# Opening of a two-layer encoder trunk: order of the first loads, first projection by token tiles, TensorE kept running on the identity

## The reference, cut to what matters

```python
# x (1, 512, 1024) float32; two layers, each: mixer, residual + layer norm, SwiGLU, residual + layer norm
proj = h @ even_w_in[0]                                   # (512, 2048): the first work
qa, ka, va, ub = jnp.split(proj, [512, 1024, 1536], axis=-1)
oa = chunk_band_attention(qa, ka, va, even_rel_bias[0])
ob = s5_mixer(ub, lam_re, lam_im, b_re, b_im, c_re, c_im, d_skip, log_dt, glu_w, glu_b)
#   dt = exp(log_dt); mag = exp(lr*dt); ar = mag*cos(li*dt); ai = mag*sin(li*dt) ... (per state)
mix = jnp.concatenate([oa, ob], axis=-1) @ even_w_out[0]
...
# layer 1: stick-breaking attention in the mixer's place
```

## Time and profile before

| | us |
|---|---|
| median of 3 runs | 1211.2 (1210.94 to 1211.3) |
| profiled execution, its own time | 1211.29 |
| span of the profiled execution (first to last instruction) | 1209.5 |
| TensorE busy | 1188.7 |
| ScalarE busy | 423.2 |
| VectorE busy | 409.7 |
| GpSimd busy | 522.2 |

### The profile page before, as it was taken

One profiled execution on the slowest core, in us unless ns is written; L12 is line 12 of the kernel. 1 busy time (PEld: TensorE's weight loads), 2 busy tenths in 40 slices (PEclk: granted clock), 3 DMA queues, 4 the chain that ended last, 5 costly groups with the idle time before them and its releaser, 6 DMA issues.

```text
span 1209.5 us, 14969 instructions
## 1 busy us (share of the span) xinstructions
PE 1188.7 (98%) x6221; PEld 970.2 (80%) x6221; DVE 409.7 (34%) x661; ACT 423.2 (35%) x577; POOL 522.2 (43%) x270
## 2 busy tenths in 40 slices
PE   7999999999999999999999999999999999999996
PEld 6877768988888888888887777778988888888885
DVE  8369462811101110000804777758211111110007
ACT  6345674332323222122225555533323222221220
POOL 6897514344444444444343222214444444444440
PEclk9999999999999999999999999999999999999998
DMA  8622315253333333233253121111633333233311
GB/s 210 184 78 68 97 66 196 67 142 98 105 88 104 87 105 104 88 105 89 62 163 87 53 70 53 53 33 56 174 93 99 91 101 104 88 105 92 101 52 70
DMA packets 152642, 117.30 MB, mean 97 GB/s; under 512 B 18688, under 2 KB 138536, under 8 KB 152576
## 3 DMA queue, kind: packets, MB, share of 16 engines
q1 hardware_dynamic: 152576, 116.36, 32.8%
HBM read 112.00 MB, written 3.17 MB: 95 GB/s over the span
## 4 chain that ended last, share of the span: by engine, by line
PE 93%; DVE 4%; ACT 1%; DMA 1%; issue 0%; SPq 0%; POOL 0%; DVEq 0%; ACTq 0%
PE ps L1480 18%; PE ps L1482 17%; PE ps L1481 17%; PE ps L1502 9%; PE ps L1504 9%; PE ps L1503 9%; PE ps L1901 2%; PE ps L1927 2%; PE ps L1912 1%; PE ps L1510 1%; PE ps L1718 1%; PE ps L1729 1%; PE ps L1945 1%; DVE stats L1353 1%; PE ps L1659 1%; PE ps L1947 1%
## 5 line engine op out<-in xcount | busy, mean ns | idle before, releaser
L571 POOL TENSOR_TENSOR wlo<-raw,whi 128x1024 fp32r<-128x1024 f32 x189 | 454.3, 2408 | 630.8 <-ACT whi L674 629.9
L1480 PE MATMUL ps<-xhi,whi 128*128 128x512 f32 (+1 forms) x1000 | 379.6, 380 | 0.0
L1482 PE MATMUL ps<-xhi,wlo 128*128 128x512 f32 (+1 forms) x1000 | 374.4, 374 | 0.0
L1481 PE MATMUL ps<-xlo,whi 128*128 128x512 f32 (+1 forms) x1000 | 374.3, 374 | 0.0
L674 ACT CAST whi<-raw 128x1024 fp32r<-128x1024 f32 x189 | 199.9, 1063 | 207.9 <-PE ps L1504 180.8
L1480 PEld LDWEIGHTS ps<-xhi,whi 128*128 128x128 f32 x1000 | 188.5, 188 | 41.0 <-issue 6.4
L1482 PEld LDWEIGHTS ps<-xhi,wlo 128*128 128x128 f32 x1000 | 188.4, 188 | 33.8
L1481 PEld LDWEIGHTS ps<-xlo,whi 128*128 128x128 f32 x1000 | 188.6, 189 | 32.3
L1022 DVE TENSOR_TENSOR gt<-ps,sg 128x512 f32<-128x512 f32 x44 | 30.4, 692 | 372.6 <-PE ps L1482 372.6
L1502 PE MATMUL ps<-whi,ghi 128*128 128x512 f32 x352 | 137.1, 390 | 0.0
L1504 PE MATMUL ps<-whi,glo 128*128 128x512 f32 x352 | 137.0, 389 | 0.0
(11 more groups left out here) (219 smaller groups left out, 1071.3 us busy)
## 6 DMA issues: line engine op xcount, KB each, us to landing
raw<-in_ffn_w SPq DMA_DIRECT2D x132, 512.0 KB, 3.8
raw<-in_odd_w_in SPq DMA_DIRECT2D x24, 512.0 KB, 3.8
raw<-in_even_w_in SPq DMA_DIRECT2D x16, 512.0 KB, 4.6
h<-in_x SPq DMA_DIRECT2D x8, 512.0 KB, 5.0
raw<-in_even_w_out SPq DMA_DIRECT2D x8, 512.0 KB, 3.6
raw<-in_odd_w_out SPq DMA_DIRECT2D x8, 512.0 KB, 3.5
bias<-rel_scratch SPq DMA_DIRECT2D x8, 256.0 KB, 4.2
out<-h SPq DMA_DIRECT2D x3, 512.0 KB, 2.6
```

What stands on the lines that cost most here:

```text
L571: eng.tensor_tensor(lo, raw_of(b), hi, ALU.subtract).then_inc(w_lo, 1)
L1480: eng.matmul(o_, w_hi_, x_hi_, start=start, stop=False)
L1481: eng.matmul(o_, w_hi_, x_lo_, start=False, stop=False)
L1482: return eng.matmul(o_, w_lo_, x_hi_, start=False, stop=stop)
```

## The change

On SyncE the first weight block is the first load, then the four x tiles; the loads of lambda and dt move to ScalarE's queue. TensorE makes 18 transposes of the identity matrix into a free PSUM bank before the first x tile. The x tiles use other PSUM banks (0, 1 for tiles 0 and 2; 4, 5 for tiles 1 and 3), so that the first projection can begin, in quarters of 128 tokens, before tile 3 is turned. ScalarE rounds block 0 and the x tiles before it makes Sin. VectorE's xlo operations stand earlier among the parameter operations. The whole diff:

```diff
--- before.py
+++ after.py
@@ -37,6 +37,7 @@
 RAW = 3
 WS = 5
 TAIL = 4
+WARM = 18
 
 ALU = mybir.AluOpType
 ACT = mybir.ActivationFunctionType
@@ -372,7 +373,7 @@
         angles, turns = psf[:, 4 * S:4 * S + PAIRS * NC], psf[:, 0:PAIRS * NC]
 
         def turned_at(n, t):
-            return 0 if n == 0 and t == 3 else 2 * t * S
+            return t % 2 * 4 * S if n == 0 else 2 * t * S
 
         def piece_cols(t, w):
             return t[:, 0:2 * w].rearrange("p (h x) -> p h x", h=2)
@@ -416,13 +417,8 @@
                     issued[0] += 1
 
             xt = x[0].rearrange("(t p) d -> t p d", p=P)
-            eng.dma_start(pl[:, 7, :], lam_re[0].rearrange("(a b) p -> a (b p)", b=2)).then_inc(lam_landed, 16)
-            eng.dma_start(pl[:, 8, :], lam_im[0].rearrange("(a b) p -> a (b p)", b=2)).then_inc(lam_landed, 16)
-            eng.dma_start(dt2[:], log_dt[0].rearrange("(a b) -> a b", b=2)).then_inc(lam_landed, 16)
-            eng.dma_start(h[:, 0, :], xt[0]).then_inc(x_landed[0], 16)
-            eng.dma_start(h[:, 1, :], xt[1]).then_inc(x_landed[1], 16)
             weights_upto(1)
-            for t in range(2, NT):
+            for t in range(NT):
                 eng.dma_start(h[:, t, :], xt[t]).then_inc(x_landed[t], 16)
             weights_upto(3)
             eng.dma_start(bnr[:], b_re[0].rearrange("(a b) p i -> (b p) a i", b=2)).then_inc(b_landed, 16)
@@ -691,21 +687,24 @@
                 eng.copy(xhi[:, :, t * P:(t + 1) * P],
                          psf[:, c:c + D].rearrange("p (k n) -> p k n", k=KT)).then_inc(x_hi, 1)
 
+            eng.dma_start(dt2[:], log_dt[0].rearrange("(a b) -> a b", b=2)).then_inc(lam_landed, 16)
+            eng.dma_start(pl[:, 7, :], lam_re[0].rearrange("(a b) p -> a (b p)", b=2)).then_inc(lam_landed, 16)
+            eng.dma_start(pl[:, 8, :], lam_im[0].rearrange("(a b) p -> a (b p)", b=2)).then_inc(lam_landed, 16)
             act.wait_ge(lam_landed, 48)
             eng.activation(dt2[:], dt2[:], ACT.Exp).then_inc(dt_ready, 1)
+            first_upper(0)
             act.wait_ge(m_ready, 1)
             eng.activation(pl[:, 4, :], pl[:, 9, :], ACT.Exp, scale=float(L)).then_inc(mag_ready, 1)
             eng.activation(scratch(MAG_), pl[:, 9, :], ACT.Exp).then_inc(mag_ready, 1)
+            first_upper(1)
+            rounded[0] = 1
+            upper_x(0, 0)
+            upper_x(0, 1)
+            upper_x(0, 2)
+            upper_x(0, 3)
             act.wait_ge(arg_ready, 1)
             eng.activation(pl[:, 16, :], pl[:, 12, :], ACT.Sin).then_inc(trig_ready, 1)
             eng.activation(pl[:, 17, :], pl[:, 13, :], ACT.Sin).then_inc(trig_ready, 1)
-            upper_x(0, 0)
-            first_upper(0)
-            upper_x(0, 1)
-            first_upper(1)
-            rounded[0] = 1
-            upper_x(0, 2)
-            upper_x(0, 3)
             upper_upto(1)
 
             def project_out(n, dst, scale=None):
@@ -1076,6 +1075,7 @@
             link(eng.tensor_scalar(q_(RS), q_(TH), PI_BELOW, -PI_BELOW, ALU.min, ALU.max))
             link(eng.scalar_tensor_tensor(out=q_(RC), in0=q_(RS), scalar=-1.0, in1=q_(RS), op0=ALU.mult, op1=ALU.min))
             eng.tensor_scalar(q_(RC), q_(RC), math.pi / 2, None, ALU.add).then_inc(arg_ready, 1)
+            lower_x(0, 0)
             count(tt(q_(A), q_(LR), q_(LR), ALU.mult))
             count(tt(q_(B), q_(LI), q_(LI), ALU.mult))
             count(eng.tensor_scalar(q_(T), q_(TH), L / (2 * math.pi), ROUNDER, ALU.mult, ALU.add))
@@ -1083,19 +1083,18 @@
             settle()
             count(tt(q_(A), q_(A), q_(B), ALU.add))
             link(eng.tensor_scalar(q_(T), q_(T), ROUNDER, None, ALU.subtract))
+            lower_x(0, 1)
             count(eng.reciprocal(q_(A), q_(A)))
             link(less(q_(TH8), q_(T), TWO_PI_1, q_(TH8)))
             link(less(scratch(TH8_), q_(T), TWO_PI_REST, q_(TH8)))
             count(eng.tensor_scalar(scratch(TURN8_), scratch(TH8_), 1 / (2 * math.pi), None, ALU.mult))
-            lower_x(0, 0)
-            lower_x(0, 1)
             settle()
             both = ps[0:PAIRS, 7, 2 * P:4 * P].rearrange("p (a b) -> p a b", a=2)
+            lower_x(0, 2)
             link(eng.tensor_copy(turn_hi[:], both))
             tt(turn_lo[:], both, turn_hi[:].bitcast(F32), ALU.subtract).then_inc(ramp_ready, 1)
 
 
-            lower_x(0, 2)
             lower_x(0, 3)
             dve.wait_ge(mag_ready, 2)
             dve.wait_ge(trig_ready, 2)
@@ -1556,16 +1555,17 @@
                     if half == 0:
                         mm.then_inc(acc_half, 1)
 
-            def project_half(half):
+            def project_quarter(t):
                 wh, wl = (w[:, 0, :].rearrange("p (k n) -> p k n", k=KT) for w in (whi, wlo))
-                c = slice(half * 2 * P, (half + 1) * 2 * P)
+                c = slice(t * P, (t + 1) * P)
+                pe.wait_ge(x_ready, t + 1)
                 for k in range(KT):
-                    if half == 0 and k == 0:
+                    if t == 0 and k == 0:
                         pe.wait_ge(first_lo, 1)
-                    if half == 0 and k == KT // 2:
+                    if t == 0 and k == KT // 2:
                         pe.wait_ge(w_lo, 1)
                     mm = three(ps[:, 2, c], wh[:, k], wl[:, k], xhi[:, k, c], xlo[:, k, c], k == 0, k == KT - 1)
-                if half:
+                if t == NT - 1:
                     mm.then_inc(w_used, 1)
 
             def project(n, b):
@@ -1575,22 +1575,28 @@
                 mm.then_inc(w_used, 1)
 
             pe.wait_ge(const_ready, 1)
-            for t in range(NT):
+            for i in range(WARM):
+                eng.transpose(ps[:, 3, 0:P], ident[:], ident[:])
+            for t in range(2):
                 pe.wait_ge(x_landed[t], 16)
-                if t == 3:
-                    pe.wait_ge(x_ready, 1)
                 turn(0, t)
-            pe.wait_ge(x_ready, 2)
-            project_half(0)
+            pe.wait_ge(x_ready, 1)
+            pe.wait_ge(x_landed[2], 16)
+            turn(0, 2)
+            project_quarter(0)
+            project_quarter(1)
+            pe.wait_ge(x_landed[3], 16)
+            turn(0, 3)
+            project_quarter(2)
             pe.wait_ge(ramp_ready, 2)
-            pe.wait_ge(x_ready, NT)
-            for row, into in enumerate((angles, turns)):
+            for row, into in ((1, turns), (0, angles)):
+                if row == 0:
+                    project_quarter(3)
                 for half in range(2):
                     c = slice(half * S, (half + 1) * S)
                     eng.matmul(into[:, c], turn_hi[:, row, :], ramp[:, c], start=True, stop=False)
                     mm = eng.matmul(into[:, c], turn_lo[:, row, :], ramp[:, c], start=False, stop=True)
             mm.then_inc(angle_done, 1)
-            project_half(1)
             pe.wait_ge(pl_ready, 1)
             for i in range(5):
                 mm = eng.transpose(ps[:, 6, i * PAIRS:(i + 1) * PAIRS], pl[:, i, :], ident[0:PAIRS, 0:PAIRS])
```

## The result

The changed kernel takes 1228.98 us as the median of four runs (1223.74 to 1232.3), the kernel before 1211.24 beside it: a ratio of 1.0143, with an interval of 1.0125 to 1.016. It is 17.7 us slower. The forecast was 1212.4, its range ended at 1215.6: the prediction is wrong, and by much more than either slow rival would explain. Slower was forecast and slower it is, but for another reason, so that much was luck. The profiled run is the shortest of the four, 1223.74 with a span of 1221.9, so its trace explains 12.45 us over the profiled run of before; the rest of the 17.7 is taken up further down.

What follows compares the result with a forecast made beforehand. TensorE, busy 98% of the span, was taken as the bound. The opening's saved 1.4 us become a wait for block 1, and late block 4 delays the third projection: +1.2 us on 1211.3 gives 1212.4, range 1210.5 to 1215.6.

Steps and rivals of the forecast that it cites:

- either slow rival: Clock stays low in the opening (1215.4 us, chance 0.20), or a 128-column matmul costs 0.11 us (1214.6, chance 0.10).
- The late block 1: Weight block 1's rest on GpSimd ready at 23.0, so the second projection starts at 23.05 against 22.88.
- A matmul of 128 columns: I take 0.067: First projection on TensorE: each 128-column matmul takes 0.067 us, a quarter 1.6 us; bounds 0.06 and 0.11.
- The rival with 0.11: First projection: a 128-column matmul costs 0.11 us, a quarter 2.7, 2.2 more than forecast, 1214.6 us; chance 0.10.
- first with a high clock from the start of the x tiles: TensorE's opening: clock at the high level from the x tiles on, their transposes 0.109 us each from about 6.5.
- The rival of the low clock: TensorE's opening: everything up to about 15 runs at half speed, 4.2 us, 1215.4 us; chance 0.20.
- Small loads on ScalarE's queue ... free: Lambda and dt loads: Exp of dt starts near 3.5 instead of 3.2, costing nothing; bounds nothing and 2 us.
- VectorE: rest of tile 0 8.75 to 9.95: VectorE's opening: rest of x tile 0 made from 8.75 to 9.95, six operations following, tile 1 ready at 12.4.
- the step that counts: TensorE turns x tile 3 only after quarter 1, to 15.0, though it has lain there since 10.4.
- the copy behind block 4: ScalarE copies the first projection after rounding block 4; third projection starts at 29.7 against 28.49, TensorE losing 1.2 us.

Runs made afterwards that it cites:

- e4: The changed kernel with each quarter as two steps of 64 columns, 192 matmuls for block 0: 1252.81 us, one run.
- e6: The kernel before with only the new order of loads, the three small loads on ScalarE's queue: 1215.14 us.
- f2: The kernel before, halves of 256 columns kept, with the angle matmuls moved behind both halves: 1211.55 us.
- e9: The kernel before with only its first projection in quarters of 128 columns; order, loads and waits untouched: 1224.12 us.
- e2: The changed kernel with the three small loads back on SyncE's queue, ahead of all other loads: 1221.96 us.
- e7: The changed kernel with GpSimd waiting for VectorE's angle arguments before it takes the first weight block: 1223.96 us.
- e5: The kernel before with only the 18 transposes of the identity added ahead of its x tiles: 1211.23 us.
- c1: The kernel before with 18 warm transposes, 16 more ahead of x tile 2, and the first projection's copy ahead of block 4's rounding: 1210.17 us.
- c2: The kernel before with 18 warm transposes and 16 more ahead of x tile 2, the copy not moved: 1211.32 us.
- e11: The changed kernel with halves, small loads first on SyncE, GpSimd's wait, and x tile 3 turned ahead of the first half: 1213.93 us.
- f1: The kernel before with quarters of 128 columns and the angle matmuls moved behind all four quarters: 1216.24 us.
- f4: The kernel before with the new order of loads and both halves of 256 columns ahead of the angle matmuls: 1213.35 us.
- f3: The changed kernel with both rows of angle matmuls moved behind all four quarters: 1229.69 us.
- e3: The changed kernel without the 18 warm transposes of the identity: 1230.3 us.
- e8: The changed kernel with halves of 256 columns, the small loads first on SyncE's queue, and GpSimd's wait for the arguments: 1216.98 us.
- e1: The changed kernel with halves of 256 columns instead of quarters, all else kept: 1219.01 us.

## Why the prediction was wrong, step by step

The second projection, forecast for 23.05, came at 33.09. The late block 1, which was to make the loss, was not waited for at all.

**"A matmul of 128 columns: I take 0.067".** This term of the sum failed first: it measured 0.111, the upper bound that I had and set aside. I reasoned from the fixed part of a matmul of 512 columns, where the weight load fits beside the streaming; at 128 it is most likely what remains (e4). The rival with 0.11 existed, at a chance of 0.10, and it was priced wrongly as well: it counted the two quarters ahead of tile 3 (2.2 us), while all four come before the second projection, 4.9 over the halves.

**"... first with a high clock from the start of the x tiles".** The forecast let the high level last once it was there, and this cost more than the term above. The rival of the low clock named only the warm-up and the wait ahead of tile 0, and neither came true: the clock was high by 7.1, and it fell behind another wait, the 5.06 us ahead of tile 2 (low from 13.9 to 17.3). The rival did not know of a fall while TensorE is busy, nor that the low level can last.

The runs show these things. The clock falls behind waits (the 5.06 us here, 2.26 us in e6, 2.29 us in f2), and it falls with TensorE busy in all four traces in which quarters with angle matmuls of 16 rows between them ran at the high level (e9, the changed kernel, e2, e7), and in one of the traces with halves that have them there (e6; not in the kernel before, e5, c1, c2 and e11). With the angle matmuls moved away that fall is gone in e9's kernel and in e6's (f1, f4); in the changed kernel the same move did not help (f3). Once low, the clock came back only in the second projection in e3, f3 and behind the busy falls of e9, e2, e7 and the changed kernel, 4 to 6 us into its matmuls of 512 columns. It came back earlier in the changed kernel at 17.3, in work of transposes and quarters, and among halves in 3.4 us (e6, e8, f4) and 6.9 us (e1). Once high, it stays so over 96 matmuls of 128 columns (f1). So quarters and the angle matmuls between them go with a fall that lasts up to the second projection, and the quarters double the number of matmuls that run at that rate; why the low level ends early in one run and late in another is open.

In e9 the clock is 8 of 13.0 us; in the changed kernel's profiled run the fall at 27.5 costs 2.8 us ahead of the second projection and 2.1 in it. That the 5 to 9 us more of its other runs are the first fall, unrecovered as in f3, fits their granted clocks but was not seen in a trace of them. A narrower tile was priced at its own duration, and never at the rate at which it and its neighbours might run.

**"Small loads on ScalarE's queue ... free".** They landed by 7.0, beyond the bound that I had set (as late as an x tile, 3.8 us after issue). The price was not the load itself but whom it held: Exp, VectorE's arguments and, in order behind them, the rest of x tile 0. e6 puts 3.9 us on the new loads alone, e2 7.0 on bringing the small ones back.

**"VectorE: rest of tile 0 8.75 to 9.95".** The order of its operations was taken over, but not their new neighbours in time. Arguments that had run beside GpSimd's preparations now meet the rest of block 0: 3.42 instead of 0.91, shown by e7.

**What held.** Block 0 landed at 4.9 (5.2 forecast) and the x tiles at 6.2 to 10.1 (6.5 to 10.4). Tile 3 behind the quarter, Sin and its table load uncovered and block 1 behind them, "the step that counts", is real: e11 takes it away and gains 3.0 us, of which some 1.7 are the fall of the clock behind the wait in e8. And the copy behind block 4 takes back what a faster opening wins (e5). Both effects were hidden in the changed kernel: TensorE was itself so late, at the low clock, that block 1's rest, ready near 30.4, was there before it was wanted at 33.09. In the changed kernel SyncE issues block 4 correspondingly late:

```profile
30.40 3.19 SPq L416 DMA_DIRECT2D raw<-in_even_w_in  x2
```

That is 9.7 us later than before, and it cost nothing further: the third projection came only behind the 24 matmuls that began at 33.09, near 41, and the copy ended at 36.3.

The range was too narrow for a plain reason. It took the cases one at a time, while the faults come together: late arguments make the wait, the clock falls behind the wait, and among the quarters it stays low over twice the number of matmuls. Mending one is therefore worth more than its share: halves, small loads and GpSimd's wait gave 10.0, 7.0 and 5.0 us alone, 22 in sum, but 12.0 together (e8).
